# Two mixers' input norm: the row scale moved onto a diagonal inside the turning products, half of the channel scales moved to ScalarE, a fourth row buffer in the second mixer

## The chip, the cores and the metric

One core of one Trainium2 chip runs the whole program. The metric is the device time of one execution in microseconds (us); the time quoted for a kernel is the median of its runs. The profile is of one further execution, taken by the hardware profiler.

## The reference, cut to what matters

Two transformer-like blocks follow each other: each has a mixer and then a mixture of 32 experts. Both mixers begin in the same way: 1024 token rows of 1024 channels (and, in the first, 256 context rows) are normalised by their root mean square, scaled and shifted per channel, and multiplied by wide projections.

```
def rmsnorm(u, w):
    uf = u.astype(jnp.float32)
    uf = uf * lax.rsqrt(jnp.mean(uf * uf, axis=-1, keepdims=True) + EPS)
    return uf.astype(u.dtype) * w

def modulate(u, shift, scale):
    return u * (1 + scale) + shift

prj_l = modulate(rmsnorm(x, norm1[layer]), sh1, sc1) @ w_in[layer]     # first block, also for ctx
...
xn = modulate_2(rmsnorm_2(h, norm1_g[l]), sh1, sc1)                    # second block
proj = xn @ w_in[l]
```

So an element needs its row's factor (one per token), its channel's factor and its channel's shift. Everything is float32.

## The kernel before, in words

`run_blocks` runs phases one after the other, and no engine goes on to the next phase before all are done: a small modulation phase, the first mixer (`mixer1_phase`, whose front is `mixer1_in`), the first mixture of experts, the second mixer (`mixer2_phase`, front `mixer2_front`) and the second mixture of experts. The change touches `mixer1_in` and `mixer2_front` only.

Both fronts work alike. The rows come in tiles of 128 tokens: `TT` = 10 of them in the first mixer (8 of `x`, 2 of `ctx`), `T` = 8 in the second. Within a tile the tokens lie on the partitions. The projections want the channels there, so each tile is turned on TensorE, in eight pieces of 128 by 128 (`J` = 8). One tile goes through these steps, and the semaphore that each one raises is in brackets:

1. SyncE loads the rows into a ring `xin` of four tiles (first mixer, where it lies in `bT`) or three (`NX`, second mixer, in `S`). A slot is loaded again once `s_xs` says that ScalarE has read its rows.
2. ScalarE squares the rows and sums them (`s_sq`).
3. VectorE adds the epsilon (`s_var`), ScalarE takes the square root (`s_sd`), VectorE the reciprocal (`s_rstd`).
4. ScalarE multiplies the 128x1024 rows by the row's factor `rstd` into `xs` (`s_xs`).
5. TensorE turns `xs` in eight transposes against the identity matrix into `pt2`, which holds two tiles in PSUM (`s_tr`). This is `tile(t)`.
6. VectorE applies the channel's factor and shift in eight 128x128 instructions, from PSUM to `tv` (`s_nev`).
7. ScalarE rounds `tv` to the high part `xh` (`s_th`).
8. VectorE subtracts, which leaves the low part `xl` (`s_tl`).

The projections are products of high and low parts: `product(n, g)` makes 24 matmuls of 512 columns (16 of them with the high weights) for 128 output channels and one group of four tiles. The order on each engine is written out by hand. On ScalarE, iteration t of the loop does the square of tile t, the row scale of tile t-1, the root of tile t and the rounding of tile t-2; iterations 2 and 3 also round the first two weight tiles (`high`). On VectorE, iteration t does epsilon and reciprocal of tile t, the channel scales of tile t-1 and the low part of tile t-2; in the first mixer iterations 3 and 4 also make the low parts of the weights (`low`), which in the second mixer are GpSimd's. The engine executes in that order, so a late instruction holds everything behind it.

TensorE's order is: tiles 0 to 5, `product(0, 0)` (which needs the low parts of tiles 0 to 3), tile 6, `product(1, 0)`, then in the first mixer tiles 7, 8 and 9, in the second tile 7, and then the products of the second group of tokens, which wait for the low part of tile 7:

```
for t in range(6):
    tile(t)
product(0, 0)
tile(6)
product(1, 0)
for t in range(7, TT):
    tile(t)
for n, g in order[2:6]:
    product(n, g)
```

From there TensorE has products enough for hundreds of microseconds.

Lines of the profile (kernel before; first mixer / second mixer): square L1265 / L2595, root L1274 / L2604, row scale L1271 / L2601, transposes L1122 / L2495, channel scales L1400 / L2784, high part L1279 / L2609, low part L1409 / L2791, epsilon and reciprocal L1392, L1394 / L2777, L2779, products L1135 to L1137 / L2369 to L2371, row loads L1090 / L2448, L2459, rounding and low part of the weights L1210, L1299 / L2354, L2359. The tiles `xs` and `tv` appear as `x_cT` in the first mixer and as `xq_S` in the second, which is also the name of the ring there.

## Time and profile before

| | us |
|---|---|
| median of 3 runs | 3145.28 (3143.79 to 3148.93) |
| profiled execution | 3146.75 |
| its span in the profile | 3145.1 |
| norm of the first mixer, first square to the product that waits for tile 7's low part | 35.8 to 91.1 |
| norm of the second mixer, the same | 1740.2 to 1791.1 |

Busy time over the span: TensorE matmuls 2760.8 us (88%), weight loads 1856.4 us, VectorE 1246.0 us, ScalarE 647.0 us, GpSimd 232.9 us. A start in the trace is counted from the span's start. A row of a timeline merges neighbouring instructions of one kind; its second number is the time from the first one's start to the last one's end. The square bracket is the idle time of that engine before it and who ended it. "PEclk" is TensorE's granted clock as a share of full speed.

### The profile page before, as it was taken

How to read it: one execution, taken by the hardware profiler on the slowest of the kernel's cores; microseconds unless marked ns; L12 is line 12 of the kernel's file. 1: busy time of each engine (PE TensorE's matmuls, PEld its weight loads, DVE VectorE, ACT ScalarE, POOL GpSimd, SP SyncE). 2: the span in 40 equal slices, each digit the busy share in tenths (PEclk: the TensorE clock that was granted, in tenths of full speed). 3: DMA queues.
4: the chain of work that ended last, by engine and by line, in shares of the span. 5: the costliest groups of instructions: out<-in, count | busy, mean ns of one | idle time of the engine just before them, and what ended most of it. 6: DMA issues, size and time to landing. Idle time of an engine off the chain costs nothing. (4 is left out here: it accounts for less than half of the span.)

```text
span 3145.1 us, 36667 instructions
## 1 busy us (share of the span) xinstructions
PE 2760.8 (88%) x13950; PEld 1856.4 (59%) x13950; DVE 1246.0 (40%) x1864; ACT 647.0 (21%) x1041; POOL 232.9 (7%) x242
## 2 busy tenths in 40 slices
PE   4999996887798899999994599899788899999993
PEld 2888775662576645544542487688666745445441
DVE  4666316885523411111114564573442611111114
ACT  3322323541302000000002422233120200000002
POOL 0000000000000000000002121121000000000002
PEclk6999997998898899999997699899898899999997
DMA  6752225779734799999996413453653699999995
GB/s 221 266 163 71 79 79 195 215 227 422 268 111 181 277 410 407 410 409 405 411 410 239 127 48 105 79 125 106 232 193 132 255 386 411 410 412 406 408 409 217
DMA packets 294746, 812.64 MB, mean 258 GB/s; under 512 B 38364, under 2 KB 160760, under 8 KB 232432
## 3 DMA queue, kind: packets, MB, share of 16 engines
q1 hardware_dynamic: 246944, 702.12, 60.0%
q10 hardware_dynamic: 32560, 63.14, 5.5%
q0 software_dynamic: 15136, 45.91, 4.2%
q8 instruction: 72, 1.18, 0.2%
q14 instruction: 34, 0.28, 0.0%
HBM read 693.18 MB, written 117.91 MB: 258 GB/s over the span
## 5 line engine op out<-in xcount | busy, mean ns | idle before, releaser
L698 PE MATMUL m_ps_y<-m_wa,m_hTa 128*128 128x512 f32 x560 | 255.5, 599 | 0.0
L677 PE MATMUL m_ps_ga<-m_wa,m_xTa 128*128 128x512 f32 x560 | 252.8, 605 | 1.0 <-issue 1.0
L687 PE MATMUL m_ps_b<-m_wb,m_xTb 128*64 128x256 f32 x2240 | 249.5, 381 | 0.0
L677 PE MATMUL m_ps_ua<-m_wa,m_xTa 128*128 128x512 f32 x560 | 246.0, 592 | 0.0
L1135 PE MATMUL xp_acc<-xp_xh,xp_wh 128*128 128x512 f32 (+3 forms) x600 | 222.1, 370 | 0.0
L1136 PE MATMUL xp_acc<-xp_xl,xp_wh 128*128 128x512 f32 (+3 forms) x600 | 220.3, 367 | 0.0
L1137 PE MATMUL xp_acc<-xp_xh,xp_wl 128*128 128x512 f32 (+3 forms) x600 | 220.2, 367 | 0.0
L687 PEld LDWEIGHTS m_ps_b<-m_wb,m_xTb 128*64 128x64 f32 x2240 | 157.8, 137 | 102.3 <-issue 26.5
L802 DVE TENSOR_TENSOR m_hida<-m_ps_ua,m_sila 128x512 f32<-128x512 f32 x35 | 24.2, 692 | 470.8 <-PE m_ps_ua L677 470.8
L770 ACT ACT_TABLE_LOAD x35 | 44.9, 1283 | 760.8 <-PE m_ps_ga L677 760.8
L2369 PE MATMUL xq_acc<-xq_xh,xq_wh 128*128 128x512 f32 x448 | 181.4, 405 | 10.3 <-DVE xq_xl L2791 5.2
L677 PEld LDWEIGHTS m_ps_ua<-m_wa,m_xTa 128*128 128x128 f32 x560 | 106.4, 190 | 133.9 <-issue 133.9
L2370 PE MATMUL xq_acc<-xq_xl,xq_wh 128*128 128x512 f32 x448 | 178.5, 398 | 0.0
L2371 PE MATMUL xq_acc<-xq_xh,xq_wl 128*128 128x512 f32 x448 | 178.3, 398 | 0.0
L677 PEld LDWEIGHTS m_ps_ga<-m_wa,m_xTa 128*128 128x128 f32 x560 | 104.8, 192 | 122.6 <-issue 120.3
L698 PEld LDWEIGHTS m_ps_y<-m_wa,m_hTa 128*128 128x128 f32 x560 | 101.0, 190 | 103.1 <-issue 100.4
L709 PE MATMUL m_ps_b<-m_wb,m_hTb 128*64 128x512 f32 x560 | 127.9, 598 | 0.0
L1135 PEld LDWEIGHTS xp_acc<-xp_xh,xp_wh 128*128 128x128 f32 (+1 forms) x600 | 112.2, 187 | 20.3 <-issue 0.6
L1137 PEld LDWEIGHTS xp_acc<-xp_xh,xp_wl 128*128 128x128 f32 (+1 forms) x600 | 111.9, 187 | 20.1
L1136 PEld LDWEIGHTS xp_acc<-xp_xl,xp_wh 128*128 128x128 f32 (+1 forms) x600 | 112.0, 187 | 19.6
L804 DVE COPY m_hTa<-m_ps_h 128x512 f32<-128x512 f32 x35 | 24.2, 692 | 243.3 <-PE m_ps_h L739 243.3
L2359 POOL TENSOR_TENSOR xq_wl<-xq_raw,xq_wh 128x1024 fp32r<-128x1024 f32 (+1 forms) x32 | 78.0, 2437 | 374.2 <-ACT xq_wh L2354 374.2
(550 smaller groups left out, 4410.9 us busy)
## 6 DMA issues: line engine op xcount, KB each, us to landing
m_wa<-in_w_dram SPq DMA_DIRECT2D x102, 1024.0 KB, 11.1
m_wb<-in_w_dram SPq DMA_DIRECT2D x102, 1024.0 KB, 11.9
m_wa<-in_w_eg_dram SPq DMA_DIRECT2D x36, 1024.0 KB, 13.3
m_wa<-in_w_eu_dram SPq DMA_DIRECT2D x36, 1024.0 KB, 11.7
m_wb<-in_w_eg_dram SPq DMA_DIRECT2D x36, 1024.0 KB, 11.7
m_wb<-in_w_eu_dram SPq DMA_DIRECT2D x36, 1024.0 KB, 15.2
m_wa<-in_w_ed_dram SPq DMA_DIRECT2D x36, 1024.0 KB, 13.4
m_wb<-in_w_ed_dram SPq DMA_DIRECT2D x36, 1024.0 KB, 15.6
```

Of the source, the lines that this page charges most:

```text
L677: last = nc.tensor.matmul(out[:, :], xT_a[:, j, :], w[:, k, :], start=(j == 0), stop=(j == J - 1))
L687: last = nc.tensor.matmul(ps_b[c * SB:(c + 1) * SB, p // 2, :], xT_b[:, j, :], w[:, k, c * HF:(c + 1) * HF], start=(j == 0), stop=(j == J ...
L698: last = nc.tensor.matmul(ps_y[:, d * NF:(d + 1) * NF], hT_a[:, k, :], w[:, c, d * NF:(d + 1) * NF], start=(k == 0), stop=(k == JF - 1))
L709: last = nc.tensor.matmul(ps_b[d * SB:(d + 1) * SB, :, :], hT_b[:, c, h * SB:(h + 1) * SB], w[:, c, d * NF:(d + 1) * NF], start=(k == 0), ...
L770: nc.scalar.activation(sil_a[:, :], ps_ga[:, :], ACT.Silu).then_inc(s_sila, 1)
L1135: nc.tensor.matmul(o, h, xh[:, j, a:a + w], start=(j == 0), stop=False)
L1136: nc.tensor.matmul(o, h, xl[:, j, a:a + w], start=False, stop=False)
L1137: last = nc.tensor.matmul(o, l, xh[:, j, a:a + w], start=False, stop=(j == J - 1))
L2359: nc.gpsimd.tensor_tensor(wl[:, n % 2, 0:k, :], raw[:, n % 2, 0:k, :], wh[:, n % 2, 0:k, :].bitcast(F32), ALU.subtract).then_inc(s_lo, 1)
L2369: nc.tensor.matmul(o, wh[:, n % 2, j, :], x_h[:, j, tok], start=(j == 0), stop=False)
L2370: nc.tensor.matmul(o, wh[:, n % 2, j, :], x_l[:, j, tok], start=False, stop=False)
L2371: last = nc.tensor.matmul(o, wl[:, n % 2, j, :], x_h[:, j, tok], start=False, stop=(j == k - 1))
```

## The change

The row factor is no longer applied by a 128x1024 instruction on ScalarE. Instead ScalarE scales the 128x128 identity matrix by `rstd` into a diagonal matrix `dgr` (two of them, in the place of `xs`), and TensorE multiplies the raw rows by that diagonal: a plain float32 matmul with the diagonal as the moving operand gives the turned and scaled piece in one. Of the eight channel scales per tile VectorE keeps the first four; the other four become ScalarE instructions with a scale and a shift per partition, just ahead of the high part. The high part waits for both halves (`s_nev`, and the new `s_nea`), and so does TensorE before it overwrites a slot of `pt2`. A slot of the row ring is now free when the tile is turned (`s_tr`) and not when ScalarE has scaled it (`s_xs`). The second mixer's ring has four tiles in place of three. The diff, of the second mixer; the first has the same edits, with a ring of four before and after, `s_col` at 2 and a second index `k` on `col` for the context:

```diff
-            NX, NR = 3, 2 * D // P + M2
+            NX, NR = 4, 2 * D // P + M2
             S = sa("S", [P, 8, D])
-            xin, xs = S[:, 0:3, :], S[:, 3:5, :]
+            xin, dgr = S[:, 0:4, :], S[:, 4, 0:2 * P].rearrange("p (r c) -> p r c", r=2)
...
                         if t >= NX:
-                            sp.wait_ge(s_xs, t - NX + 1)
+                            sp.wait_ge(s_tr, t - NX + 1)
                         sp.dma_start(xin[:, t % NX, :], h_t[t]).then_inc(s_x[t % NX], 16)
...
                         if t >= 2:
                             pe.wait_ge(s_nev, t - 1)
+                            pe.wait_ge(s_nea, t - 1)
                         for j in range(J):
-                            last = nc.tensor.transpose(pt2[:, t % 2, j, :], xs[:, t % 2, j::J], ident[:, :])
+                            last = nc.tensor.matmul(pt2[:, t % 2, j, :], xin[:, t % NX, j::J], dgr[:, t % 2, :], start=True, stop=True)
                         last.then_inc(s_tr, 1)
...
+                    act.wait_ge(s_mask, 1)
                     for t in range(T + 2):
...
-                            nc.scalar.activation(xs[:, u % 2, :], xin[:, u % NX, :], ACT.Copy, scale=rstd[:, u:u + 1]).then_inc(s_xs, 1)
+                            nc.scalar.activation(dgr[:, u % 2, :], ident[:, :], ACT.Copy, scale=rstd[:, u:u + 1]).then_inc(s_xs, 1)
...
                         if t > 1:
+                            if t == 2:
+                                act.wait_ge(s_col, 1)
+                            if t >= 4:
+                                act.wait_ge(s_tl, t - 3)
+                            act.wait_ge(s_tr, t - 1)
+                            for j in range(J // 2, J):
+                                last = nc.scalar.activation(tv[:, t % 2, j, :], pt2[:, t % 2, j, :], ACT.Identity, scale=col[:, 0, j:j + 1], bias=col[:, 2, j:j + 1])
+                            last.then_inc(s_nea, 1)
+                            act.wait_ge(s_nea, t - 1)
                             act.wait_ge(s_nev, t - 1)
                             nc.scalar.activation(xh[:, :, (t - 2) * P:(t - 1) * P], tv[:, t % 2, :, :], ACT.Copy).then_inc(s_th, 1)
...
                             v.wait_ge(s_tr, b + 1)
-                            for j in range(J):
+                            for j in range(J // 2):
                                 last = nc.vector.tensor_scalar(tv[:, b % 2, j, :], pt2[:, b % 2, j, :], col[:, 0, j:j + 1],
                                                                col[:, 2, j:j + 1], ALU.mult, ALU.add)
```

How ScalarE's instructions stand now. Here is the first mixer's loop before, from the row scale of iteration 3 to the high part of iteration 4 (row scale, root, the weights' high part, high part, square; the bracket is the semaphore waited for):

```order
L1271 ACTIVATE x_cT<-x_bT,xp_rstd 128x1024 [waits xp_tr,xp_rstd]
L1274 ACTIVATE xp_rstd<-xp_ss 128x1 [waits xp_var]
L1210 ACTIVATE xp_wh<-xp_raw 128x1024 [waits xp_raw1]
L1279 ACTIVATE xp_xh<-x_cT 128x8x128 [waits xp_nev]
L1265 ACTIVATE xp_ob,xp_ss<-x_bT 128x1024 [waits xp_sq,xp_x0]
L1271 ACTIVATE x_cT<-x_bT,xp_rstd 128x1024 [waits xp_tr,xp_rstd]
L1274 ACTIVATE xp_rstd<-xp_ss 128x1 [waits xp_var]
L1279 ACTIVATE xp_xh<-x_cT 128x8x128 [waits xp_nev]
```

and in the changed kernel, the same stretch:

```order
L1273 ACTIVATE x_cT<-x_ident,xp_rstd 128x128 [waits xp_tr,xp_rstd]
L1276 ACTIVATE xp_rstd<-xp_ss 128x1 [waits xp_var]
L1211 ACTIVATE xp_wh<-xp_raw 128x1024 [waits xp_raw1]
L1287 ACTIVATE x_cT<-xp_pt,xp_col 128x128 [waits xp_tr]
L1287 ACTIVATE x_cT<-xp_pt,xp_col 128x128 x3
L1291 ACTIVATE xp_xh<-x_cT 128x8x128 [waits xp_nev,xp_nea]
L1267 ACTIVATE xp_ob,xp_ss<-x_bT 128x1024 [waits xp_sq,xp_x0]
L1273 ACTIVATE x_cT<-x_ident,xp_rstd 128x128 [waits xp_tr,xp_rstd]
L1276 ACTIVATE xp_rstd<-xp_ss 128x1 [waits xp_var]
L1287 ACTIVATE x_cT<-xp_pt,xp_col 128x128 [waits xp_tr,xp_tl]
L1287 ACTIVATE x_cT<-xp_pt,xp_col 128x128 x3
L1291 ACTIVATE xp_xh<-x_cT 128x8x128 [waits xp_nev,xp_nea]
```

The row scale has become a 128x128 instruction, four channel scales stand between the root and the high part, and the line numbers moved by a few.

TensorE, tile 5 of the first mixer and the first products behind it, before:

```order
L1122 MATMUL xp_pt<-x_ident,x_cT 128x128 [waits xp_nev,xp_xs]
L1122 MATMUL xp_pt<-x_ident,x_cT 128x128 x7
L1135 MATMUL xp_acc<-xp_xh,xp_wh 128x512 [waits xp_tl,xp_lo]
L1136 MATMUL xp_acc<-xp_xl,xp_wh 128x512
L1137 MATMUL xp_acc<-xp_xh,xp_wl 128x512
L1135 MATMUL xp_acc<-xp_xh,xp_wh 128x512
```

and after:

```order
L1123 MATMUL xp_pt<-x_cT,x_bT 128x128 [waits xp_nea,xp_nev,xp_xs]
L1123 MATMUL xp_pt<-x_cT,x_bT 128x128 x7
L1136 MATMUL xp_acc<-xp_xh,xp_wh 128x512 [waits xp_tl,xp_lo]
L1137 MATMUL xp_acc<-xp_xl,xp_wh 128x512
L1138 MATMUL xp_acc<-xp_xh,xp_wl 128x512
L1136 MATMUL xp_acc<-xp_xh,xp_wh 128x512
```

The moving operand is the diagonal in place of the identity, the stationary one comes from the ring of rows (`x_bT`), and each tile waits for one semaphore more. SyncE's row loads of the first mixer (with two weight tiles, and the bias behind them), before:

```order
L1090 DMA x_bT<-in_x_dram 128x1024
L1073 DMA xp_raw<-in_w_in_dram 128x8x128
L1090 DMA x_bT<-in_x_dram 128x1024
L1090 DMA x_bT<-in_x_dram 128x1024 [waits xp_xs] x4
L1090 DMA x_bT<-in_ctx_dram 128x1024 [waits xp_xs] x2
L1097 DMA xp_bias<-in_dt_bias_dram 128x32
```

and after:

```order
L1090 DMA x_bT<-in_x_dram 128x1024
L1073 DMA xp_raw<-in_w_in_dram 128x8x128
L1090 DMA x_bT<-in_x_dram 128x1024
L1090 DMA x_bT<-in_x_dram 128x1024 [waits xp_tr] x4
L1090 DMA x_bT<-in_ctx_dram 128x1024 [waits xp_tr] x2
L1097 DMA xp_bias<-in_dt_bias_dram 128x32
```

The same loads stand in the same places and wait for the turned tile.

## Rows read from the trace of the kernel before

**Rows 1.** Waits of TensorE from 1791 us on: us in total, times, longest.

```profile
PE xq_acc L2369 <- DVE xq_xl L2791: 5.2, 1, 5.2
```

**Rows 2.** Windows: us, busy per engine, PEclk, DMA share, GB/s.

```profile
150.00:250.00 100.00, 100.00 (x558) 87.39 (x557) 63.94 (x59) 28.62 (x37) 0.00 (x0) 1.00 0.49 157
1740.00:1772.00 32.00, 12.44 (x53) 10.37 (x54) 20.81 (x63) 21.51 (x34) 4.71 (x2) 0.50 0.62 188
```

**Rows 3.** Timeline of ScalarE, second mixer: start, us, line, shape, idle before.

```profile
1748.22 1.06 ACT L2595 ACTIVATE xq_S<-xq_S 128x1024 f32<-128x1024 f32 x1 [1.34 <-DMA xq_S<-stage]
...
1761.83 0.20 ACT L2604 ACTIVATE xq_rstd<-xq_ss 128x1 f32<-128x1 f32 x1 [1.17 <-DVE xq_ss L2777]
1761.94 1.04 ACT L2609 ACTIVATE xq_xh<-xq_S 128x1024 fp32r<-128x1024 f32 x1
1762.88 1.04 ACT L2595 ACTIVATE xq_S<-xq_S 128x1024 f32<-128x1024 f32 x1
...
1763.92 1.13 ACT L2601 ACTIVATE xq_S<-xq_S,xq_rstd 128x1024 f32<-128x1024 f32 x1
...
1771.12 0.20 ACT L2604 ACTIVATE xq_rstd<-xq_ss 128x1 f32<-128x1 f32 x1 [1.17 <-DVE xq_ss L2777]
```

**Rows 4.** Timeline of TensorE, second mixer: tiles 4 and 5.

```profile
1765.11 1.97 PE L2495 MATMUL xq_pt<-x_ident,xq_S 128*128 128x128 f32 x8 [2.43 <-ACT xq_S L2601]
1770.00 1.97 PE L2495 MATMUL xq_pt<-x_ident,xq_S 128*128 128x128 f32 x8 [2.92 <-ACT xq_S L2601]
```

**Rows 5.** Timeline of VectorE, second mixer, between those tiles.

```profile
1767.12 2.65 DVE L2784 TENSOR_SCALAR xq_S<-xq_pt,xq_col 128x128 f32<-128x128 f32 x8
1769.68 1.21 DVE L2791 TENSOR_TENSOR xq_xl<-xq_S,xq_xh 128x1024 fp32r<-128x1024 f32 x1
```

**Rows 6.** ScalarE's groups by form: busy us, mean ns of one.

```profile
L1611 ACT ACTIVATE ss_w<-ss_w,x_lnd 128x128 f32<-128x128 f32 x256 | 76.4, 387 | 30.7 <-DVE ss_w L1666 30.7
L2379 ACT ACTIVATE xq_ob<-xq_acc,xq_bcol 128x512 f32<-128x512 f32 x32 | 22.0, 688 | 119.7 <-PE xq_acc L2371 119.7
L1222 ACT ACTIVATE xp_xpad<-xp_acc 128x512 f32<-128x512 f32 x32 | 19.1, 599 | 123.6 <-PE xp_acc L1137 123.6
L238 ACT ACTIVATE m_lT<-m_ps_q 36x128 f32<-36x128 f32 x16 | 4.3, 270 | 12.4 <-PE m_ps_q L290 12.4
```

**Rows 7.** Timeline of ScalarE, first mixer: third square; two evictions in a row.

```profile
44.18 1.06 ACT L1265 ACTIVATE xp_ob<-x_bT 128x1024 f32<-128x1024 f32 x1 [2.66 <-DMA x_bT<-in_x_dram]
...
94.81 1.07 ACT L1222 ACTIVATE xp_xpad<-xp_acc 128x512 f32<-128x512 f32 x2
```

**Rows 8.** Timeline of TensorE: eight transposes, then plain float32 products.

```profile
75.40 1.05 PE L1122 MATMUL xp_pt<-x_ident,x_cT 128*128 128x128 f32 x8
...
603.50 1.05 PE L1550 MATMUL ss_cb<-x_cT,x_bT 128*128 128x128 f32 x8
...
619.01 3.75 PE L1559 MATMUL ss_o<-x_cT,ss_hst 128*128 128x128 f32 x16 [4.99 <-DVE ss_yo L1699]
```

**Rows 9.** Timeline of TensorE, first mixer: tiles 5 and 9.

```profile
67.07 1.97 PE L1122 MATMUL xp_pt<-x_ident,x_cT 128*128 128x128 f32 x8 [3.97 <-ACT x_cT L1271]
...
89.08 1.97 PE L1122 MATMUL xp_pt<-x_ident,x_cT 128*128 128x128 f32 x8 [4.16 <-ACT x_cT L1271]
```

**Rows 10.** Timeline of TensorE, second mixer: tile 7 and the products behind it.

```profile
1784.86 1.05 PE L2495 MATMUL xq_pt<-x_ident,xq_S 128*128 128x128 f32 x8
1791.14 0.79 PE L2369 MATMUL xq_acc<-xq_xh,xq_wh 128*128 128x512 f32 x1 [5.23 <-DVE xq_xl L2791]
...
1792.59 0.63 PE L2369 MATMUL xq_acc<-xq_xh,xq_wh 128*128 128x512 f32 x1
...
1795.49 0.40 PE L2371 MATMUL xq_acc<-xq_xh,xq_wl 128*128 128x512 f32 x1
```

**Rows 11.** Windows: plain products with idle time between them.

```profile
485.00:491.00 6.00, 3.75 (x8) 2.52 (x8) 5.46 (x5) 3.98 (x14) 0.00 (x0) 0.50 0.15 36
497.00:503.00 6.00, 3.54 (x8) 2.52 (x8) 3.38 (x4) 0.00 (x0) 0.00 (x0) 0.65 0.37 128
```

More of the change, by code:

```diff
@@ L1033, in mixer1_in @@
         xin = bT
-        xs, tv = cT[:, 0:2, :], cT[:, 2:4, :].rearrange("p r (j c) -> p r j c", j=J)
+        dgr, tv = cT[:, 0, 0:2 * P].rearrange("p (r c) -> p r c", r=2), cT[:, 2:4, :].rearrange("p r (j c) -> p r j c", j=J)
         junk = ob[:, 0:2, :].rearrange("p a b -> p (a b)")
@@ L1045, in mixer1_in @@
             sem(k) for k in ("one", "mask", "cin", "ct", "cw", "par", "col", "din"))
-        s_sq, s_var, s_sd, s_rstd, s_xs, s_tr, s_nev, s_th, s_tl = (
-            sem(k) for k in ("sq", "var", "sd", "rstd", "xs", "tr", "nev", "th", "tl"))
+        s_sq, s_var, s_sd, s_rstd, s_xs, s_tr, s_nev, s_nea, s_th, s_tl = (
+            sem(k) for k in ("sq", "var", "sd", "rstd", "xs", "tr", "nev", "nea", "th", "tl"))
         s_hi, s_lo, s_mm, s_ev, s_pad, s_cv, s_ch, s_xc, s_tq, s_te, s_link = (
@@ L1088, in _ @@
                     if t >= 4:
-                        sp.wait_ge(s_xs, t - 3)
+                        sp.wait_ge(s_tr, t - 3)
                     sp.dma_start(xin[:, t % 4, :], x_t[t] if t < T else c_t[t - T]).then_inc(s_x[t % 4], 16)
@@ L1120, in tile @@
                         pe.wait_ge(s_nev, t - 1)
+                        pe.wait_ge(s_nea, t - 1)
                     for j in range(J):
-                        last = nc.tensor.transpose(pt2[:, t % 2, j, :], xs[:, t % 2, j::J], ident[:, :])
+                        last = nc.tensor.matmul(pt2[:, t % 2, j, :], xin[:, t % 4, j::J], dgr[:, t % 2, :], start=True, stop=True)
                     last.then_inc(s_tr, 1)
@@ L1270, in _ @@
                             act.wait_ge(s_tr, v - 1)
-                        nc.scalar.activation(xs[:, v % 2, :], xin[:, v % 4, :], ACT.Copy, scale=rstd[:, v:v + 1]).then_inc(s_xs, 1)
+                        nc.scalar.activation(dgr[:, v % 2, :], ident[:, :], ACT.Copy, scale=rstd[:, v:v + 1]).then_inc(s_xs, 1)
                     if t < TT:
@@ L1277, in _ @@
                     if t > 1:
+                        k = int(t - 2 >= T)
+                        if t == 2:
+                            act.wait_ge(s_col, 2)
+                        if t >= 4:
+                            act.wait_ge(s_tl, t - 3)
+                        act.wait_ge(s_tr, t - 1)
+                        for j in range(J // 2, J):
+                            last = nc.scalar.activation(tv[:, t % 2, j, :], pt2[:, t % 2, j, :], ACT.Identity, scale=col[:, k, 0, j:j + 1], bias=col[:, k, 2, j:j + 1])
+                        last.then_inc(s_nea, 1)
+                        act.wait_ge(s_nea, t - 1)
                         act.wait_ge(s_nev, t - 1)
@@ L2413, in mixer2_front @@
                 sem(k) for k in ("one", "mask", "zf", "cin", "ct", "cw", "in", "ls", "pp", "par", "col"))
-            s_sq, s_var, s_sd, s_rstd, s_xs, s_tr, s_nev, s_th, s_tl = (
-                sem(k) for k in ("sq", "var", "sd", "rstd", "xs", "tr", "nev", "th", "tl"))
+            s_sq, s_var, s_sd, s_rstd, s_xs, s_tr, s_nev, s_nea, s_th, s_tl = (
+                sem(k) for k in ("sq", "var", "sd", "rstd", "xs", "tr", "nev", "nea", "th", "tl"))
             s_w, s_l, s_bs, s_b, s_c, s_wm, s_cv, s_ca, s_cx, s_cd = (
@@ L2493, in tile @@
                             pe.wait_ge(s_nev, t - 1)
+                            pe.wait_ge(s_nea, t - 1)
                         for j in range(J):
-                            last = nc.tensor.transpose(pt2[:, t % 2, j, :], xs[:, t % 2, j::J], ident[:, :])
+                            last = nc.tensor.matmul(pt2[:, t % 2, j, :], xin[:, t % NX, j::J], dgr[:, t % 2, :], start=True, stop=True)
                         last.then_inc(s_tr, 1)
@@ L2588, in drain @@
                                 act.dma_start(za_dram[m * P:(m + 1) * P, :, :], zob[:, m % 2, :, :]).then_inc(s_z[m % 2], 16)
+                    act.wait_ge(s_mask, 1)
                     for t in range(T + 2):
@@ L2607, in _ @@
                         if t > 1:
+                            if t == 2:
+                                act.wait_ge(s_col, 1)
+                            if t >= 4:
+                                act.wait_ge(s_tl, t - 3)
+                            act.wait_ge(s_tr, t - 1)
+                            for j in range(J // 2, J):
+                                last = nc.scalar.activation(tv[:, t % 2, j, :], pt2[:, t % 2, j, :], ACT.Identity, scale=col[:, 0, j:j + 1], bias=col[:, 2, j:j + 1])
+                            last.then_inc(s_nea, 1)
+                            act.wait_ge(s_nea, t - 1)
                             act.wait_ge(s_nev, t - 1)
@@ L2782, in _ @@
                             v.wait_ge(s_tr, b + 1)
-                            for j in range(J):
+                            for j in range(J // 2):
                                 last = nc.vector.tensor_scalar(tv[:, b % 2, j, :], pt2[:, b % 2, j, :], col[:, 0, j:j + 1],
```

## The prediction

> **What bounds the kernel now.** I read the windows first, then the waits of TensorE, then the timelines of the two norm stages, engine by engine. The reader is to see in the windows that the products behind the norm fill TensorE (100.00 us busy of 100 in one stretch), while in the second mixer's norm it is busy 12.44 of 32 us, at a granted clock of 0.50 [rows 2]. A time won in the products would count on TensorE; a time won in the norm counts by how much earlier the products can start. From 1791 us to the end of that norm's products the one wait on these tiles is that of 5.2 us for the low part of tile 7 [rows 1].
>
> What sets the norm's pace is a chain through three engines. Follow it from one root to the root two tiles later: root at 1761.83, high part at 1761.94, square at 1762.88, row scale at 1763.92 [rows 3], turning of tile 4 at 1765.11 [rows 4], channel scales at 1767.12, low part at 1769.68 [rows 5], epsilon, next root at 1771.12 [rows 3]. No step waits for an earlier engine than the one named before it, and the sum is 9.29 us for two tiles. The steps are 0.11 (root), 0.94 (high part), 1.04 (square), 1.19 (row scale to the tile's start), 2.01 (turning), 2.56 (channel scales), 1.44 (low part, epsilon and hand-over).
>
> **The prices.** *The diagonal.* A 128x128 ScalarE instruction with a pointer operand lasts 387 ns, and 256 of them in rows took 76.4 us, 0.30 each [rows 6]. From its start to the tile's start I take 0.387 and the 0.06 of hand-over that stand between 1763.92 + 1.13 and 1765.11 [rows 3, 4]: 0.45 in place of 1.19, **-0.74**.
>
> *The channel scales on VectorE.* Eight start and end in 2.56 us, so four take 1.28, **-1.28**.
>
> *The channel scales on ScalarE.* No row shows an instruction that has both a scale and a shift per partition, so I bound it. Two PSUM evictions of 512 columns take 1.07 us, one lasts 0.60 [rows 6, 7], so the second begins 0.47 after the first. At 128 elements one lasts 0.27, 0.33 less, which leaves 0.14 between starts. One pointer operand costs 688 - 599 = 89 ns [rows 6]. Lower end: the pointers hide, 0.14. Upper end: nothing overlaps, 0.27 + 0.18 = 0.45. I take two pointers at 0.09 each, since rows 6 show one at that price: 0.14 + 0.18 = 0.32 between starts, 0.45 for the last. Four take 3 x 0.32 + 0.45 + 0.06 of hand-over to the high part, which now waits for them: 1.47, **+1.47**. They stand between root and high part, so the square, the next diagonal and the next tile are queued behind them.
>
> The Trainium skill ("ScalarE: Activation LUTs", What ACT_TABLE_LOAD costs) says that each pointer operand adds about 93 ns; the rows agree for one pointer (89 ns), and no row shows two.
>
> *The product.* A plain float32 product of 128x128 costs no more than a transpose: eight take 1.05 us, as eight transposes do, and sixteen take 3.75 at the lower clock, where eight transposes take 1.97 [rows 4, 8]. So 0. The same rows answer a rule that speaks against this change: the Trainium skill ("TensorE: Matmul & The Clock Gate", Terms) calls the transpose mode four times faster for float32. By that rule the turning would be dearer by far (a rival below); the rows here contradict it.
>
> *Waits and queues.* The row ring is freed about 2 us later (after the turning). In the first mixer a slot turned at tile t-4 is squared again at tile t, three tiles of some 4.6 us later; in the second the fourth slot gives one more tile. SyncE is held by that wait, and with it the first mixer's bias and third weight tile queued behind, which nothing needs before the second group of products. If this cover went, each late row would push the chain by its lateness, at most the 2 us. The second mixer's tile 3 is loaded earlier, behind the weight tile in the same queue: 0. TensorE's new wait for tile t-2's second half cannot bind, because ScalarE makes the diagonal of tile t after it.
>
> **The sum.** Per two tiles the chain becomes 9.29 - 0.74 - 1.28 + 1.47 = 8.74, only 0.55 less. Where the products start, by the walk from the last load that is waited for:
>
> - Second mixer, to tile 5. The third square starts at 1748.22 [rows 3], the diagonal of tile 1 1.06 later, the root by 1749.65. Then root 0.11, weights' high part 0.94 (same form as the high part), four scales 1.47, high part and hand-over 1.10, low part to next root 1.44: root of tile 3 at 1754.71. Then 0.11 + 0.94 + 1.47 + 0.94 + 1.04 + 0.45 = 4.95: tile 3 at 1759.66. Then 2.01 + 1.28 + 1.44: root of tile 5 at 1764.39; then 0.11 + 1.47 + 0.94 + 1.04 + 0.45 = 4.01: tile 5 at 1768.40, where it was 1770.00 [rows 4]. **-1.6.**
> - First mixer, to tile 5. The same walk from 44.18 [rows 7], 1704.04 earlier, with one low part of a weight tile (1.2, the form of rows 5) on VectorE more: 1768.40 - 1704.04 + 1.2 = 65.56, where it was 67.07 [rows 9]. **-1.5.**
> - First mixer, tile 7 to tile 9. The same terms as one turn of the chain: **-0.5** on 89.08 [rows 9].
> - Second mixer, end of tile 7 (1784.86 + 1.05) to the product at 1791.14: 5.23 [rows 10]. Now 0.06 + 1.47 (ScalarE's four, longer than VectorE's) + 1.10 + 1.21 + 0.06 = 3.90. **-1.3.**
>
> Together -4.9 us. The profiled execution took 3146.75, so this one would take 3141.85; it lies 1.5 us above the median of the runs shown, and on the median the forecast is 3145.28 - 4.9 = **3140.4 us**. What is late next is ScalarE: 0.30 + 0.11 + 1.47 + 0.94 + 1.04 = 3.9 us a tile against a pace of 4.4.
>
> The cost of one scale instruction enters some 32 times (three fours before tile 5 and one behind, in each mixer). At 0.14 the sum is -10.7 (less where VectorE's part then binds), at 0.45 it is -0.7.
>
> **The rivals.** A measurement of this kernel can tell 0.2%, 6.3 us, from no change.
>
> - *The second pointer is free.* For: the rows price only one. Then 0.23 each, 32 x 0.09 = 2.9 us more: -7.8, **3137.5**. 18%.
> - *ScalarE's scales do not overlap.* At 0.45 the gain is gone but for 0.7: **3144.6**. For: they read PSUM while VectorE does. Against: the evictions of rows 7 overlap. 10%.
> - *The clock.* In the norm the granted clock is 0.50, the lower of the two levels (1.2 GHz). With plain products it might be granted in full. Then tiles 3 and 5 of each mixer and tile 9 take 1.05 in place of 1.97 (5 x 0.92 = 4.6), and the products start at the higher level: behind the norm about nine of them last 0.63 in place of 0.40 [rows 10], nine times 0.2 is 1.8, at four starts 7. Sum -4.9 - 4.6 - 7 = -16.5: **3128.8**. Against: plain products busy 3.75 of 6 us were granted 0.50, and only the third such burst saw it rise (0.65) [rows 11]; the norm is busy 2 of 4.4; and a wait of 4.16 us goes with a tile at the lower level [rows 9], so 3.9 probably does too. 7%. This is also what the Trainium skill would have ("TensorE: Matmul & The Clock Gate", Part 4: PE-mode transpose), which says that transposes do not count as TensorE's activity: plain products would then count where these did not, and no run here has shown it.
> - *The turning becomes dearer* (the other side). If a plain product with the raw rows as weights cost four times a transpose, eight would take 4 x 1.97 = 7.9 us at the lower level (+5.9) and 4.2 at the higher (+3.2). Five tiles at the lower level are on the path and four between products (6 and 7 of each mixer): 29.5 + 12.8 = 42, less 4.9: +37, **3182**. It decides from where 72 products are dearer by 4.9 us, 68 ns each. Against: the equal times of eight [rows 8]. 3%. It is the rule of the Trainium skill named under *The product*.
> - *The change does nothing*, because a load that I take for granted sets the pace (the third tile's row wait at 44.18 and 1748.22 repeated by later tiles): 3145. 3%.
>
> **How the numbers follow.** The forecast has 59%. Faster by over 0.2% (below 3139.0): the free pointer, the clock, and a small part of the forecast's own scatter: 0.28. Slower: the dear turning and a piece of scatter: 0.05. Within 0.2%: 0.67. The range reaches from a price near the lower end, -10.8, to the upper end and a scatter of about 1 us on either side: 3134.5 to 3146.0; it leaves the clock and the dear turning out.
>
> **What would show it.** Right: the four ScalarE scales of a tile start 0.32 apart and last 0.45; the tiles' starts lie 4.4 us apart on average and not 4.65; TensorE's wait before the second mixer's product is 3.9 us; ScalarE's idle time before roots nearly gone; eight turning products still 1.97 us at clock 0.50; no table load among the scales. Wrong: a turning above 2.1 us; ScalarE waiting for rows in later tiles; a PEclk above 0.6 in the norm; starts of the products earlier, yet the same end, which would mean that some wait after the norm was not tied to it.

## The result: slower by 17.8 us, where 4.9 less were forecast

The changed kernel took **3162.35 us** (median of 6 runs, 3159.98 to 3167.54). The kernel before, timed beside it, took 3144.53 (6 runs, 3141.81 to 3148.93). The ratio is **1.0054**, with a 95% interval of 1.0045 to 1.0064. The forecast was 3140.4, in a range of 3134.5 to 3146.0. The profiled execution's span is 3160.4 us, 15.3 more than that of the profiled execution before (3145.1).

Where did the time come in? Count each norm from the start of its first square on ScalarE to the first product of its third group of 24, the one that waits for tile 7's low part; behind it TensorE has work enough. These starts are read from the timelines of one profiled execution of each kernel.

| first square to ... | first mixer before, after | second mixer before, after |
|---|---|---|
| first group of products | 32.89, 36.66 | 31.41, 36.40 |
| second group | 40.39, 45.92 | 39.09, 45.68 |
| third group | 55.25, 64.97 | 50.93, 59.20 |

The norms lost 9.72 and 8.27 us. That is 18.0 together, as much as the medians differ (17.8). So nothing after the norms is needed to explain it. The rest of the program varies from one profiled execution to the next: between the two norms (first mixer's third group to second mixer's first square) it takes 1649.15 us before and 1645.39 after, and over the kernels below whose expert blocks have the same work it lies between 1643.6 and 1652.4. Sums over the norms can therefore miss a profiled total by several us.

The page of the changed kernel counts 144 matmuls more than the page before (13950 there):

```profile
PE 2797.8 (89%) x14094; PEld 1896.8 (60%) x14094; DVE 1223.0 (39%) x1792; ACT 660.8 (21%) x1113; POOL 231.9 (7%) x242
```

The norms turn 18 tiles of eight blocks, 144 blocks, and the change was to replace one instruction by one. So each of them is recorded as two. The groups by form show the same. The first two lines are the turning in the first mixer, as matmuls and as weight loads; the other two are ScalarE's and VectorE's halves of the channel scales in the second.

```profile
L1123 PE MATMUL xp_pt<-x_cT,x_bT 128*128 128x128 f32 x160 | 40.5, 429 | 16.2 <-ACT x_cT L1273 16.2
L1123 PEld LDWEIGHTS xp_pt<-x_cT,x_bT 128*128 128x128 f32 x160 | 38.8, 334 | 17.8 <-ACT x_cT L1273 17.7
L2628 ACT ACTIVATE xq_S<-xq_pt,xq_col 128x128 f32<-128x128 f32 x32 | 12.0, 453 | 10.1 <-PE xq_pt L2508 10.1
L2807 DVE TENSOR_SCALAR xq_S<-xq_pt,xq_col 128x128 f32<-128x128 f32 x32 | 10.9, 405 | 29.5 <-PE xq_pt L2508 29.5
```

The first mixer turns ten tiles of eight blocks, so 80 products are issued, and 160 are recorded. A plain float32 product runs as two matmuls with a weight load each, where a transpose ran as one [rows 4, 8].

The timeline of TensorE, first mixer, tiles 2 to 9 (start, us, then what it waited for before):

```profile
50.91 4.18 PE L1123 MATMUL xp_pt<-x_cT,x_bT 128*128 128x128 f32 x16 [2.65 <-ACT x_cT L1273]
56.04 4.17 PE L1123 MATMUL xp_pt<-x_cT,x_bT 128*128 128x128 f32 x16 [0.94 <-ACT x_cT L1273]
63.07 4.19 PE L1123 MATMUL xp_pt<-x_cT,x_bT 128*128 128x128 f32 x16 [2.86 <-ACT x_cT L1273]
68.18 4.18 PE L1123 MATMUL xp_pt<-x_cT,x_bT 128*128 128x128 f32 x16 [0.92 <-ACT x_cT L1273]
77.68 3.85 PE L1123 MATMUL xp_pt<-x_cT,x_bT 128*128 128x128 f32 x16
86.84 7.66 PE L1123 MATMUL xp_pt<-x_cT,x_bT 128*128 128x128 f32 x32
```

And the second mixer, tiles 2 to 7, with the products behind the last:

```profile
1761.80 4.09 PE L2508 MATMUL xq_pt<-xq_S 128*128 128x128 f32 x16 [2.31 <-ACT xq_S L2615]
1767.26 4.18 PE L2508 MATMUL xq_pt<-xq_S 128*128 128x128 f32 x16 [1.37 <-ACT xq_S L2615]
1772.72 4.19 PE L2508 MATMUL xq_pt<-xq_S 128*128 128x128 f32 x16 [1.28 <-ACT xq_S L2615]
1778.28 4.17 PE L2508 MATMUL xq_pt<-xq_S 128*128 128x128 f32 x16 [1.36 <-ACT xq_S L2615]
1787.79 3.86 PE L2508 MATMUL xq_pt<-xq_S 128*128 128x128 f32 x16
1796.98 3.86 PE L2508 MATMUL xq_pt<-xq_S 128*128 128x128 f32 x16
1804.92 0.80 PE L2381 MATMUL xq_acc<-xq_xh,xq_wh 128*128 128x512 f32 x1 [4.08 <-DVE xq_xl L2814]
```

A tile took 1.97 us alone in the norm and 1.05 between products [rows 4, 8, 10]. It now takes 4.18 and 3.86. Two tiles come in 1772.72 - 1761.80 = 10.92 us. The forecast's chain of 8.74 with 4.18 in place of 1.97 gives 10.95. So this one term accounts for the pace.

ScalarE and VectorE between two roots of the second mixer, the rows that answer to [rows 3, 5]:

```profile
1768.65 0.20 ACT L2618 ACTIVATE xq_rstd<-xq_ss 128x1 f32<-128x1 f32 x1 [1.44 <-DVE xq_ss L2800]
1768.76 1.49 ACT L2628 ACTIVATE xq_S<-xq_pt,xq_col 128x128 f32<-128x128 f32 x4
1770.28 1.06 ACT L2632 ACTIVATE xq_xh<-xq_S 128x1024 fp32r<-128x1024 f32 x1
1771.25 1.04 ACT L2609 ACTIVATE xq_S<-xq_S 128x1024 f32<-128x1024 f32 x1
...
1772.29 0.39 ACT L2615 ACTIVATE xq_S<-x_ident,xq_rstd 128x128 f32<-128x128 f32 x1
1774.20 0.20 ACT L2618 ACTIVATE xq_rstd<-xq_ss 128x1 f32<-128x1 f32 x1 [1.53 <-DVE xq_ss L2800]
```

```profile
1771.48 1.37 DVE L2807 TENSOR_SCALAR xq_S<-xq_pt,xq_col 128x128 f32<-128x128 f32 x4 [2.43 <-PE xq_pt L2508]
1772.77 1.22 DVE L2814 TENSOR_TENSOR xq_xl<-xq_S,xq_xh 128x1024 fp32r<-128x1024 f32 x1
```

The change saved what it was meant to: the diagonal takes 0.39 us where the row scale took 1.13, and VectorE's four scales take 1.37, with the next instruction 1.29 after their start, where eight took 2.65. VectorE then waits for TensorE (2.43 us), and ScalarE's root for VectorE (1.44 and 1.53).

### The profile page after: what moved, and what is told of

It reads as the page before. It is cut to its first block and busy times, and to the rows that moved or that the text cites. A ratio compares the mean times of both kernels' runs of the same rounds, so it can differ in the third digit from the quotient of the medians.

```text
span 3160.4 us, 36991 instructions
## 1 busy us (share of the span) xinstructions
PE 2797.8 (89%) x14094; PEld 1896.8 (60%) x14094; DVE 1223.0 (39%) x1792; ACT 660.8 (21%) x1113; POOL 231.9 (7%) x242
## 5 line engine op out<-in xcount | busy, mean ns | idle before, releaser
L698 PE MATMUL m_ps_y<-m_wa,m_hTa 128*128 128x512 f32 x560 | 255.5, 599 | 0.0
L698 PEld LDWEIGHTS m_ps_y<-m_wa,m_hTa 128*128 128x128 f32 x560 | 101.1, 190 | 103.2 <-issue 100.4
## 6 DMA issues: line engine op xcount, KB each, us to landing
m_wa<-in_w_eu_dram SPq DMA_DIRECT2D x36, 1024.0 KB, 11.7
```

The source lines that it names most:

```text
L698: last = nc.tensor.matmul(ps_y[:, d * NF:(d + 1) * NF], hT_a[:, k, :], w[:, c, d * NF:(d + 1) * NF], start=(k == 0), stop=(k == JF - 1))
```

## The experiments

Each kernel differs from its parent by the edit shown. The times are medians with the ratio to the kernel before, timed beside them, and its interval. Two kernels change the data (noted there), and with it how many expert blocks of the MoE stage have work. Their totals are therefore not compared with the others, only their norms. The norms' times, first square to third group:

| kernel | first mixer | second mixer | ratio |
|---|---|---|---|
| before | 55.25 | 50.93 | 1 |
| after | 64.97 | 59.20 | 1.0054 [1.0045, 1.0064] |
| e1, after with transposes | 51.39 | 48.64 | 0.9992 [0.9983, 1.0001] |
| e2, after, neighbouring channels | 57.63 | 54.84 | (other data) |
| e3, before with the split | 55.46 | 50.14 | 1.0008 [0.9998, 1.0018] |
| e4, after without the split | 64.66 | 60.74 | 1.0061 [1.0047, 1.0075] |
| e6, before with plain products | 67.38 | 63.40 | 1.0057 [1.0044, 1.0070] |
| e7, before, neighbouring channels | 54.70 | 51.33 | (other data) |

### Only the transposes put back

```diff
-  matmul(pt2[:, t % 2, j, :], xin[:, t % 4, j::J], dgr[:, t % 2, :], start=True, stop=True)
+  transpose(pt2[:, t % 2, j, :], xin[:, t % 4, j::J], ident[:, :])
```

The diagonal is still written and waited for, but the row factor is missing from the result. The expert blocks have as much work as before (560 matmuls in the group of L698, as there), so the total can be compared.

> The changed kernel, but the eight pieces of a tile are turned by transposes of the raw rows against the identity (the diagonal is still made, the row factor is left out of the result). Theory (the turning is what costs: in the trace of the changed kernel each plain product runs as two matmuls, 16 a tile, 4.18 us in place of 1.97): the tile takes 1.97 us again and the forecast's sum comes true, about 4.9 us faster than the kernel before, near 3140. Rival (ScalarE's four channel scales in the chain are what costs): still slower than before by 10 us or more, 3155 or above.

3142.57 us (3136.71 to 3146.25, 11 runs) beside 3144.56. Everything else of the change is in place, and the loss is gone: the norms take 51.39 and 48.64, which is 3.9 and 2.3 us less than before. Tiles 3 and 5 of the second mixer:

```profile
1756.16 1.98 PE L2508 MATMUL xq_pt<-x_ident,xq_S 128*128 128x128 f32 x8 [3.13 <-ACT xq_S L2615]
...
1764.96 1.97 PE L2508 MATMUL xq_pt<-x_ident,xq_S 128*128 128x128 f32 x8 [2.67 <-ACT xq_S L2615]
```

That is 8.80 us for two tiles; the forecast's chain was 8.74. This is the kernel that the prediction described, with the product at 0. In total it gained 2 us, with an interval that includes none, where the norms show 6.2 in the one profiled execution.

### Only the product put in

```diff
-  transpose(pt2[:, t % 2, j, :], xs[:, t % 2, j::J], ident[:, :])
+  matmul(pt2[:, t % 2, j, :], xs[:, t % 2, j::J], ident[:, :], start=True, stop=True)
```

> The kernel before with one edit: the eight transposes of a tile become eight plain float32 products of the same scaled rows with the identity; nothing else moves. Theory A (the product alone is what was mis-sized: two matmul records each, each with a strided load of 312 to 338 ns): a tile takes 4.18 us instead of 1.97 at the lower clock and 3.85 instead of 1.05 at full clock, x16 records a tile, and the time is before plus 18 to 26 us, that is 3163 to 3171; a little above the kernel with the diagonal alone (ratio 1.0061), since the row scale of 1024 columns stays. Theory B (the loss came of the diagonal: of its being written late, or of the waits that moved with it): a tile of products takes no longer than 2.5 us here, and the time is within 3 us of before. Theory C (the plain product is dear, but only behind raw rows that no engine has just written): the tile is between the two and the time before plus 5 to 12.

3163.45 us (3161.72 to 3168.98, 5 runs) beside 3146.71: +16.7, by the ratio +17.9. Theory A holds. The time lies at the lower end of its range (18 to 26 us above), so it asked somewhat too much. The expectation that this kernel lies above the one with the diagonal alone did not show: 1.0057 and 1.0061 can't be told apart, though its norms are 2.7 us longer each. (The profiled execution was the slowest of the five: its span is 22.3 us longer than before's, and its norms 24.6.) The tile and its loads are those of the changed kernel:

```profile
L1122 PEld LDWEIGHTS xp_pt<-x_ident,x_cT x160: 311/336/342, 40.3 to 101.8; 128*128 128x128 f32 x160
L1122 PE MATMUL xp_pt<-x_ident,x_cT x160: 277/442/607, 40.3 to 102.0; 128*128 128x128 f32 x160
```

(Min, median and max in ns.) Here no diagonal exists, the rows are scaled as before, and no wait has moved. The plain product alone makes a loss of the size measured.

### The split alone, the diagonal alone

The split of e3 is the diff's part with `s_nea` and `J // 2`, put into the kernel before. e4 is the changed kernel with that part taken out:

```diff
-  pe.wait_ge(s_nea, t - 1)
-  for j in range(J // 2, J): activation(tv[:, t % 2, j, :], pt2[:, t % 2, j, :], ...)
-  for j in range(J // 2):
+  for j in range(J):
       last = nc.vector.tensor_scalar(tv ...
```

> The kernel before with one part of the change: four of eight channel scales on ScalarE; row scale, transposes, ring and its release as before. From the rows (four on ScalarE 1.49 us in the chain, four fewer on VectorE -1.28): two tiles of the chain 9.5 us in place of 9.3, the wait behind tile 7 of the second mixer 1.3 shorter; together within 1 us of the kernel before, 3145. Rival (ScalarE's scales cost the 17 us): 3155 or above.

3147.60 us (3143.95 to 3155.07, 11 runs) beside 3144.56: by the ratio +2.5, with an interval from -0.6 to +5.7 that includes none. ScalarE now runs through without idle time between roots:

```profile
1763.61 0.20 ACT L2616 ACTIVATE xq_rstd<-xq_ss 128x1 f32<-128x1 f32 x1
1763.72 1.49 ACT L2626 ACTIVATE xq_S<-xq_pt,xq_col 128x128 f32<-128x128 f32 x4
...
1768.28 0.18 ACT L2616 ACTIVATE xq_rstd<-xq_ss 128x1 f32<-128x1 f32 x1
```

From root to root it takes 4.67 us, which is what the norm took per tile before (4.65). The split alone only exchanges the chain for ScalarE.

> The changed kernel without the split: all eight channel scales on VectorE, row scale on the diagonal, ring of four and its release after the turning. Theory (turning): two tiles of the chain 9.29 - 0.74 + 2.2 = 10.75 us, time within 3 us of the changed kernel, 3162 to 3165. Rival (ScalarE's scales): near the kernel before, 3145.

3164.03 us (3161.84 to 3167.17, 5 runs). Tiles 3 and 5 of the second mixer start 10.74 us apart (1769.85, 1780.59), where 10.75 was expected. The loss comes with the product, split or not; the intervals of 1.0061 and 1.0054 overlap.

### The stride of the weights

```diff
-  matmul(pt2[:, t % 2, j, :], xin[:, t % 4, j::J], dgr[:, t % 2, :], start=True, stop=True)
+  matmul(pt2[:, t % 2, j, :], xin[:, t % 4, j * P:(j + 1) * P], dgr[:, t % 2, :], start=True, stop=True)
```

The channels land in other places of the turned tile, so another function is computed: 544 matmuls in the group of the expert blocks' L698, where before has 560. This is why its 3116.47 us says nothing of the change.

> The changed kernel, but the raw rows are the weights of a product in pieces of 128 neighbouring channels, not every eighth one (channels land in other places, the work is the same). Theory a (the spacing of 0.24 us at either clock comes from the strided float32 weight load of 336 ns): loads near 190 to 230 ns, 16 matmuls in 3.75 us at the lower clock and in 2.05 at the higher, so about 0.4 us less per tile of the chain and 1.8 less per tile that stands among products: 8 to 12 us faster than the changed kernel, near 3152. Theory b (only the doubled count costs): loads stay at 336 ns, time as the changed kernel's, 3162.

Theory a holds: at full clock a load takes 192 ns in place of 335, and 16 matmuls take 1.95 us in place of 3.85. At the lower clock they take 3.78 in place of 4.18.

The same edit on the kernel before, whose transposes then read neighbouring channels (also 544):

> The kernel before, but each transpose reads 128 neighbouring channels where it read every eighth (the channels land in other places of the turned tile, so the numbers of the result change, and with them how many expert blocks have work). It gives the missing cell: transposes of neighbouring channels. If the stride costs transposes nothing, a tile stays at 1.97 us at the lower clock and 1.05 at full clock. If a strided transpose is load-bound as the strided product is, it falls: weight loads from 186 to 231 down to 140 or so, a tile at full clock to 0.8 or 0.9 us.

The single run took 3107.67 us, with other data as well. A tile stays at 1.97 and 1.04 us, so the stride costs the transposes nothing, although their loads do become shorter.

Loads and matmuls between products, where the granted clock is high, of e2:

```profile
L1123 PEld LDWEIGHTS xp_pt<-x_cT,x_bT x64: 188/192/333, 74.8 to 93.2; 128*128 128x128 f32 x64
L1123 PE MATMUL xp_pt<-x_cT,x_bT x64: 270/275/576, 75.0 to 93.4; 128*128 128x128 f32 x64
```

of the changed kernel, and of the kernel before:

```profile
L1123 PEld LDWEIGHTS xp_pt<-x_cT,x_bT x63: 312/335/338, 77.4 to 99.8; 128*128 128x128 f32 x63
```

```profile
L1122 PEld LDWEIGHTS xp_pt<-x_ident,x_cT x32: 186/193/230, 75.2 to 90.4; 128*128 128x128 f32 x32
```

and of e7:

```profile
L1122 PEld LDWEIGHTS xp_pt<-x_ident,x_cT x29: 137/141/230, 73.9 to 88.7; 128*128 128x128 f32 x29
```

With the tiles' durations from the timelines this fills a table (us for eight blocks, lower clock and full clock):

| | neighbouring channels | every eighth channel |
|---|---|---|
| transposes | 1.97, 1.04 | 1.97, 1.05 |
| plain products | 3.78, 1.95 | 4.18, 3.85 |

Neighbouring, a product takes 1.9 times a transpose at either clock, as its two matmuls say. At full clock the stride lengthens the transposes' loads from 141 to 193 ns, and the tile does not get longer. It lengthens the plain products' loads from 192 to 335, and a record then begins every 0.24 us where it began every 0.11 (median distance of two starts). At the lower clock the spacing is the same 0.24 with the stride, and 0.21 without, but the loads are as long either way. These are e2's there:

```profile
L1123 PEld LDWEIGHTS xp_pt<-x_cT,x_bT x48: 202/333/337, 51.0 to 65.9; 128*128 128x128 f32 x48
```

So the spacing of strided products does not follow the clock. That it follows from the stride is shown (e2); by what step inside the load is not, since a recorded load of 333 ns goes with either spacing.

The 18.0 us of the norms now come apart. Strided transposes to products of neighbouring channels (e2 less e1; the stride's own part in it is nothing, by e7: -0.55 and +0.40 us) cost 6.24 + 6.20 = **12.4**. The stride (after less e2) costs 7.34 + 4.36 = **11.7**. The rest of the change (e1 less before) gives back 3.86 + 2.29 = **6.2**.

### Can the clock help?

In the norm before TensorE is granted the lower level [rows 2]. I filled its idle time with products of the identity with itself into a part of the accumulator that is written anew later; nobody reads them. On the kernel before:

```diff
+  def busy(n):
+      for _ in range(n): matmul(acc[:, 3, 0:P], ident[:, :], ident[:, :], start=True, stop=True)
+  busy(18)
   for t in range(6):
       tile(t)
+      if t < 5: busy(11)
...
   tile(8)
+  busy(10)
```

(12 ahead of tile 0 and ahead of the last products in the second mixer.)

> The kernel before with idle time of TensorE in both norms filled by products of the identity with itself, whose result nobody reads (18, 12 ahead of tile 0, 11 after each of tiles 0 to 4, 10 to 12 ahead of the last products). They test whether the clock or the loads set a transposing tile and the first products. Theory clock: TensorE is granted the higher clock in both norms, a tile of transposes takes 1.05 instead of 1.97 us (0.9 us in each turn of a loop that passes through it) and the first products start at the higher clock: minus 5 to minus 12 us, 3133 to 3140. Rival: the extra products stand ahead of the tile in TensorE's queue and delay it by up to 1 us each time, as rows come late anyway: 0 to plus 5 us, and the granted clock rises all the same.

**3137.05 us** (3130.65 to 3138.97, 5 runs), ratio **0.9968** [0.9955, 0.9980]. The windows (columns as in [rows 2]) and a tile with its filling:

```profile
1740.00:1772.00 32.00, 27.99 (x203) 25.83 (x203) 24.68 (x70) 23.71 (x37) 4.74 (x2) 0.97 0.58 181
```

```profile
1755.20 1.16 PE L2504 MATMUL xq_pt<-x_ident,xq_S 128*128 128x128 f32 x8 [1.74 <-ACT xq_S L2618]
1756.20 2.62 PE L2556 MATMUL xq_acc<-x_ident 128*128 128x128 f32 x22
...
1764.59 0.47 PE L2378 MATMUL xq_acc<-xq_xh,xq_wh 128*128 128x512 f32 x1
```

The clock is 0.97 where it was 0.50, a tile lasts 1.16 in place of 1.97, and the first product behind tile 5 lasts 0.47 (before 0.77, at 1771.62). Eleven filling products count 22 records: the doubling again, here with neighbouring weights. To the third group the norms take 53.47 and 48.10, 4.6 us less than before together; the runs show about 10 us less, by the interval 6.3 to 14. The two profiled spans differ by 8.9: besides the norms 1.15 lie ahead of the first square, 2.6 between the norms and 0.6 behind them, which is within what these stretches vary by from one execution to the next. So 4.6 us are traced to the filling, and the rest is not. Totals of before scatter from 3140.66 to 3152.51.

The same on the changed kernel, with four products between tiles:

> The changed kernel with the same filling, shorter (four products of the identity between tiles, since less idle time is left). Theory (the tile of products is bound by strided loads that no clock shortens): at full clock a tile still takes 3.85 us, 0.33 less than at the lower clock, and the time falls by 2 to 7 us below the changed kernel's 3162: 3155 to 3160, still above before. Rival (the tile is slow because of the lower clock): tiles fall to 2.1 us, and the time to before's or below, 3140 to 3146.

```profile
60.00:100.00 40.00, 36.81 (x165) 34.19 (x165) 17.80 (x41) 23.85 (x55) 0.00 (x0) 0.96 0.62 225
```

```profile
57.22 4.08 PE L1123 MATMUL xp_pt<-x_cT,x_bT 128*128 128x128 f32 x16 [0.99 <-ACT x_cT L1282]
61.13 1.06 PE L1187 MATMUL xp_acc<-x_ident 128*128 128x128 f32 x8
63.31 4.08 PE L1123 MATMUL xp_pt<-x_cT,x_bT 128*128 128x128 f32 x16 [1.12 <-ACT x_cT L1282]
```

3166.60 us (3161.51 to 3170.88, 6 runs), ratio 1.0060 [1.0045, 1.0076]: no gain, and the forecast of 2 to 7 us less missed. At a granted clock of 0.88 (30 to 60 us) and 0.96 a tile still takes 4.08, so the 3.85 expected missed too: that is what a tile takes between products. The rival falls: the clock does not shorten the strided tile by more than 0.1 us, and the norms are 1.4 us longer each than the changed kernel's (66.36 and 60.57).

### The row scale on GpSimd

The other way to free ScalarE keeps the transposes:

```diff
-  nc.scalar.activation(xs[:, v % 2, :], xin[:, v % 4, :], ACT.Copy, scale=rstd[:, v:v + 1]).then_inc(s_xs, 1)
+  nc.gpsimd.tensor_scalar(xs[:, t % 2, :], xin[:, t % 4, :], rstd[:, t:t + 1], None, ALU.mult).then_inc(s_xs, 1)
```

In the second mixer GpSimd also makes the low parts of the first two weight tiles; they now stand behind its row scales of tiles 3 and 5.

> The kernel before with the row scale (rows times their own factor) on GpSimd instead of ScalarE, transposes kept, channel scales all on VectorE. It frees 1.2 us of ScalarE a tile. If GpSimd scales 128x1024 float32 in under 2.4 us and is not held by VectorE on the way, the pace a tile falls from 4.65 to about 4.4 us (VectorE's statistics and eight scales), and the time by 2 to 6 us: 3139 to 3143. If its instruction takes 3 us or more, it stands in the chain root, row scale, tile in place of 1.2 us, and the time is before plus 5 to 15. The low halves of two tiles in the second mixer stand behind it in GpSimd's queue; if they come late the product of that mixer starts later, which would show as a loss in the second mixer only.

3146.88 us (3141.49 to 3151.37, 11 runs), ratio 1.0001 [0.9992, 1.0010]. The 2.84 us of its instruction lie between the two cases of the expectation, and so does the time. GpSimd's group (1740 to 1800 us) and one turn:

```profile
L2449 POOL TENSOR_SCALAR xq_S<-xq_S,xq_rstd 128x1024 f32<-128x1024 f32 x8 | 22.8, 2844 | 12.8 <-DVE xq_rstd L2785 12.8
```

```profile
1758.94 0.20 ACT L2610 ACTIVATE xq_rstd<-xq_ss 128x1 f32<-128x1 f32 x1 [2.54 <-DVE xq_ss L2783]
...
1762.33 1.97 PE L2504 MATMUL xq_pt<-x_ident,xq_S 128*128 128x128 f32 x8 [1.28 <-POOL xq_S L2449]
```

From root to tile it is 3.39 us. Before it was 3.28 (1761.83 to 1765.11, [rows 3, 4]), by way of high part, square and row scale in ScalarE's queue. The slower engine begins earlier and ends no earlier.

With the split of the channel scales as well:

> The row scale on GpSimd and the channel scales split four and four between VectorE and ScalarE, transposes kept. If GpSimd is short enough, the split now costs ScalarE nothing that the row scale had not taken (1.49 against 1.21 us), VectorE loses 1.28 us of its 4.4, and the pace a tile is 3.9 to 4.2 us: 9 tiles of one mixer and 8 of the other give minus 7 to minus 12 us, 3133 to 3138. If GpSimd's instruction paces the chain (3 us or more), this and the one without the split end at the same time within 3 us.

3140.70 us (3135.07 to 3151.20, 12 runs), ratio 0.9985 [0.9974, 0.9995]. ScalarE now has room for its four scales. Tiles 4 and 5 of the second mixer come 4.16 us apart (1763.36, 1767.52), as expected, but tiles 3 and 4 come 6.97 apart (1756.39, 1763.36): there VectorE's low part takes 3.08 us in place of 1.23, while GpSimd makes the low part of a weight tile (last section). Of the 7 to 12 us expected about 5 came. The norms are 4.7 and 1.4 us shorter than before, so less of the gain arrives in the second mixer, where those low parts are GpSimd's. That they alone take it is not shown.

Both with the filling (nine products between tiles), and the filling with the split alone:

> The kernel before with the row scale on GpSimd, the channel scales split four and four, and idle time of TensorE in both norms filled with products of the identity with itself. Alone, the first two together measured 0.9985 and the filling alone 0.9968. If they add up (the one shortens the chain ahead of TensorE, the other TensorE's own part of it): 0.9953, that is minus 14 to 15 us, 3129 to 3133. If they overlap, because the filled TensorE holds up tiles that now come every 4.15 us: no better than the filling alone, 3135 to 3138.

> The kernel before with the filling and the split of the channel scales, row scale still on ScalarE. The split alone measured 1.0008: ScalarE's own work paces the loop there. With the filling the tile takes 1.16 instead of 1.97 us, so the chain through TensorE is still shorter and ScalarE's sum still the longer: the same as the filling alone within 2 us, 3134 to 3138. If the split was held by the chain through TensorE instead, it now gains 3 us or more: under 3133.

f3 took **3133.47 us** (3129.95 to 3137.33, 6 runs), ratio **0.9955** [0.9940, 0.9970]: the sum of its parts (0.9968 and 0.9985 make 0.9953), and faster than both kernels of this case. f4 took 3138.56 (3131.17 to 3143.91, 12 runs), 0.9976 [0.9966, 0.9986]: with the filling the split adds nothing on ScalarE, as without it (its median lies just above the 3134 to 3138 expected). The intervals of f1 and f3 overlap, so that GpSimd and split are worth something on top of the filling is not shown by them alone.

## Why the prediction was wrong

- **The product** is the step that failed: "A plain float32 product of 128x128 costs no more than a transpose: eight take 1.05 us, as eight transposes do". The row of L1550 says x8 [rows 8], and I took these for eight products. The loop there issues four (one for each of the `G` = 4 groups), and the group of L1550 has 128 matmuls in 16 chunks: eight records for four products. The row of L1559 says x16 for eight. So the rows priced a product at two transposes, 0.26 us at full clock and 0.47 at the lower. A second thing the rows did not have: L1550 reads neighbouring weights. In place of 0 the term measured +2.2 us a tile at the lower clock and +2.8 at the higher: 12.4 us for the doubling and 11.7 for the stride in the norms. By the forecast's own count (five tiles on the path at the lower clock, four between products) it is 5 x 2.2 + 4 x 2.8 = 22.2 us; less the 4.9 saved that leaves 17.3, where 17.8 were measured.
- **The dear turning** was the right rival, at 3%. Its size, 37 us by four times a transpose at both clocks, was too much: it is 2.1 times at the lower clock and 3.7 at the higher. The Trainium skill ("TensorE: Matmul & The Clock Gate", Terms), which says that the transpose mode is four times faster for float32, was dismissed on the misread row; the traces come near it at full clock with strided weights only (3.7), and with neighbouring ones the factor is 1.9.
- **The diagonal** (-0.74): right. 0.39 us each.
- **VectorE's four scales** (-1.28): right. 1.37 from first start to last end, the next instruction 1.29 after the first start.
- **ScalarE's four scales** (+1.47, 0.32 apart, 0.45 the last): right. One lasts 450 to 453 ns, four take 1.49, so they start (1.49 - 0.45)/3 = 0.35 apart. With a free second pointer the starts would be 0.23 apart, without overlap 0.45: both rivals fall.
- **The sum without the product** (-4.9): the chain was right (8.80 for two tiles in e1, forecast 8.74), and so was TensorE's wait before the second mixer's last products (forecast 3.9, measured 4.08). e1's norms show -6.2; its total, 2 us less with an interval that ends at none, agrees less well.
- **The clock**: the granted clock of the changed kernel's norms did rise, to 0.66 (1740 to 1772 us), and the tiles in this stretch still took 4.09 to 4.18 us. So this rival's condition came about in part, and its gain did not. That filling idle time raises the clock was shown on the kernel before. That the chip counts a transpose as less than a product isn't shown by this: the plain products also keep TensorE busy longer (17.01 of these 32 us, where it was 12.44).
- **The row ring and the new waits** at 0: right. After the third tile no square waits for a load in the second mixer.

The range left out what a misread count could cost, since it was made from ScalarE's price alone.

## What to carry to other kernels

Before a duration is taken from a group's row, divide its count by what the loop issues: a plain float32 product is two matmuls with a weight load each, a transpose one. In this kernel a product that replaced a transpose to save a pass over the rows took about twice as long, and 3.7 times where the turned operand was read with a stride at full clock. Where TensorE idled in a short chain, filling it paid when the chain held transposes (0.32%), and did not when it held strided products.

## What the runs showed that I had not expected

- The plain products' strided load lasts 335 ns at either clock, where the transposes' takes 193 at full clock with the same addresses (e1).
- Where TensorE is busy 12.44 of 32 us [rows 2], products that nobody reads gained 0.32%.
- GpSimd's row scale (2.84 us, one SBUF tensor) does not hold up VectorE, but its low part of a weight tile (two SBUF tensors) does. The low part of a tile on VectorE takes 1.22 us under the first. Under the second it takes 2.03, and ends 1.08 us after the second has ended (1762.24 + 2.35 = 1764.59):

```profile
1757.50 1.22 DVE L2797 TENSOR_TENSOR xq_xl<-xq_S,xq_xh 128x1024 fp32r<-128x1024 f32 x1
...
1763.64 2.03 DVE L2797 TENSOR_TENSOR xq_xl<-xq_S,xq_xh 128x1024 fp32r<-128x1024 f32 x1
```

```profile
1756.18 2.84 POOL L2449 TENSOR_SCALAR xq_S<-xq_S,xq_rstd 128x1024 f32<-128x1024 f32 x1
...
1762.24 2.35 POOL L2361 TENSOR_TENSOR xq_wl<-xq_raw,xq_wh 128x1024 fp32r<-128x1024 f32 x1
```

  The Trainium skill ("SBUF — State Buffer", Terms) calls the port pair of these two engines an exclusive lock that is held for the whole instruction. The second of each pair of rows agrees: 1764.59 to the end at 1765.67 leaves 1.08 us for the instruction that waited, and in the kernel with the split (1756.31 + 2.36 to 1756.67 + 3.08) it is 1.08 as well. The other order agrees too: where VectorE's low part began first (1752.77, 1.21 us), GpSimd's took 3.36 us from 1752.84 on, in place of 2.35. The first of each pair does not agree: VectorE's instruction ran its 1.22 us inside GpSimd's 2.84, both reading SBUF, and neither got longer. So by these runs the lock does not hold for GpSimd's row scale.
